# Six slots for weight pieces instead of four: the low part is written over the raw weights, and TensorE frees the slot

## The chip, the cores and the metric

The kernel runs on one core of a Trainium2 chip. The metric is the device time of one execution in microseconds (us). Five engines run their own instruction streams beside each other and meet only at semaphores: TensorE (PE, with its weight load PEld), VectorE (DVE), ScalarE (ACT), GpSimd (POOL) and SyncE (SP), which here issues nearly all DMA transfers. On-chip memory (SBUF) has 128 partitions.

## The reference

Two decoder layers on 256 tokens of width 2048, all in float32. Cut to what matters, one layer is:

```
h = rms_norm(x, norm_mix) * (1 + sc_a) + sh_a        # sc, sh, gates: c_act @ ada_w + ada_b
cq, ckv, ... = split(h @ w_in)                       # one wide projection
o_mla, o_fox, o_nsa = three attention mixers         # nsa also compresses k and v:
                                                     #   gelu(blocks @ cmp_w1) @ cmp_w2
x = x + gt_a * (concat(rms_norm(o_...)) @ w_out)
h = rms_norm(x, norm_mlp) * (1 + sc_m) + sh_m
x = x + gt_m * (square(relu(h @ mlp_w1)) @ mlp_w2)   # d_ff = 8192
```

Every weight is read once, so the kernel streams some 630 MB from HBM past a small activation (256 tokens).

## The kernel before, in words

**Pieces.** All large weights are cut into 828 pieces of 256 rows by up to 512 columns (512 KB), 414 for each layer: 158 for the attention part (`ORDER`, line 38 on) and 256 for the MLP. `PIECES` lists them in the order in which TensorE uses them. A float32 product is made of three products in the fp32r format: each weight piece is split into a high part `w_hi` (a rounding copy) and a low part `w_lo` (raw minus high), and the activations are split in the same way.

**The life of piece Q.** SP loads it into `w_raw[Q % RING]` (`load_piece`, lines 591 to 610). ACT makes `w_hi` (`hi`, line 713) once the load has landed and TensorE has used piece Q - RING (`piece_used`). DVE makes `w_lo` (`lo`, line 1150) once `hi_done` says so. TensorE multiplies (`product`, line 1600: 12 matmuls in most pieces; `compress`, line 1642: 4 matmuls for the pieces called `cw1`), then raises `piece_used`. RING is 4, and each of `w_raw`, `w_hi` and `w_lo` has four slots of its own. The raw slot is free again when `lo` of piece Q - 4 is done (`lo_done`, line 608).

**Side work in a written order.** ACT runs `hi(Q)` and then the side steps listed for Q, DVE runs `lo(Q)` and then its side steps for Q: turning transposed blocks out of PSUM, softmax units (`slot`), evacuations, residuals, and the adaLN modulation. A transpose that TensorE does behind piece Q is taken out at Q + 3 (`t_step` calls with `F + q + 3`), so at such places ACT and DVE cannot be more than some three pieces ahead of TensorE. Within the side steps of one Q the adaLN tile comes last (priority 5 in `ada_block`).

**The adaLN tiles.** `c_act @ ada_w` has one row, and DVE does it: 384 tiles of 128 x 1024 raw values (512 KB each) are loaded by SP and added into `ada_acc` (line 1092). The first 64 use eight slots in `arena`, the rest two slots `ada_raw`; a tile's load waits until DVE has used the tile two before it (`ada_used`). In the attention part of layer 0 and in its MLP the tiles are dense, later they are few, and in the attention part none stands behind a `cw1` piece.

**SP's queue.** SP issues weight and tile loads from one list, `LOADS` (lines 361 to 372), in order and blocking: a load that waits holds back all behind it. The list is sorted by the place in DVE's order at which the load's buffer comes free: for piece Q that is `lo` of Q - 4, for a tile the tile two before it.

**Stages.** Start (norm of layer 0 and its first chunks, with 64 tiles): up to about 182 us. The stretch with the `cw1` pieces, which alternate with others: 182 to 346 us in layer 0 and 1430 to 1582 us in layer 1. The rest of the attention part follows each. MLP of layer 0: some 579 to 1330 us. MLP of layer 1: from some 1810 us to the end.

Of the kernel before, what the change touches and what calls it, by code (L numbers as in the profile page):

```python
# [6 lines left out]
F32 = mybir.dt.float32  # L7
F32R = mybir.dt.float32r
# [5 lines left out]
P = 128  # L14
# [42 lines left out]
SUPERS = 4  # L57
MLP_LEN = SUPERS * 64
LAYER = FRONT + MLP_LEN
RING = 4  # L60
ALL = LAYERS * LAYER


# [294 lines left out]
assert len(ADA_LAST) == len(ADA_BLOCKS)  # L358


DVE_AT = {e: i for i, e in enumerate(DVE_ORDER)}
LOADS = []
for Q in range(ALL):
    free = DVE_AT["lo", Q - RING] if Q >= RING else DVE_AT["ada", 8 + Q]
    LOADS.append((free, DVE_AT["lo", Q], "w", Q))
for n in range(TILES):
    if n < FIRST_TILES:
        free = DVE_AT["ada", n - FIRST_RING] if n >= FIRST_RING else -1
    else:
        free = DVE_AT["ada", n - 2] if n >= FIRST_TILES + 2 else DVE_AT["ada", n - FIRST_RING]  # L370
    LOADS.append((free, DVE_AT["ada", n], "ada", n))
LOADS.sort()
# [34 lines left out]
def trunk(nc, x, c, positions, inv_freq, ada_w, ada_b, norm_mix, norm_mlp, w_in, fox_b_f, mla_q_norm, mla_w_uq,  # L407
          mla_kv_norm, mla_w_ukv, nsa_pos_k, nsa_pos_v, cmp_k_w1, cmp_k_w2, cmp_v_w1, cmp_v_w2,
          out_norm, w_out, mlp_w1, mlp_w2, final_norm, out):
    with ExitStack() as ctx:  # L410
        def sb(name, shape, dt=F32):
            return ctx.enter_context(nc.sbuf_tensor(name, shape, dt))

        def sem(name):
            return ctx.enter_context(nc.semaphore(name))
# [2 lines left out]
        X = sb("X", [P, 2, D])  # L418
        hT_hi, hT_lo = sb("hT_hi", [P, KT, SEQ], F32R), sb("hT_lo", [P, KT, SEQ], F32R)
        uT_hi, uT_lo = sb("uT_hi", [P, KT, SEQ], F32R), sb("uT_lo", [P, KT, SEQ], F32R)  # L420
        w_raw = sb("w_raw", [P, RING, 2, 512])
        w_hi, w_lo = sb("w_hi", [P, RING, 2, 512], F32R), sb("w_lo", [P, RING, 2, 512], F32R)
        ada_raw = sb("ada_raw", [P, 2, 1024])
        ada_acc = sb("ada_acc", [P, 1024])
        ybuf = sb("ybuf", [P, 2, 2, 512])
# [77 lines left out]
        packed, c_landed, loaded, consts, x_landed = sem("packed"), sem("c_landed"), sem("loaded"), sem("consts"), sem("x_landed")  # L503
        raw_landed = [sem(f"raw_landed{i}") for i in range(RING)]
        hi_done, lo_done, piece_used = sem("hi_done"), sem("lo_done"), sem("piece_used")
# [83 lines left out]
        @block.sync  # L589
        def _(sp):  # L590
            def load_piece(Q):
                l, chunk, p = PIECES[Q]
                if type(chunk) is not str:
                    s, ch = chunk
                    if ch < 4:
                        src = mlp_w1[l, 256 * p:256 * p + 256, s * D + 512 * ch:s * D + 512 * ch + 512]
                    else:
                        src = mlp_w2[l, s * D + 256 * p:s * D + 256 * p + 256, 512 * (ch - 4):512 * (ch - 4) + 512]
                    n = 512
                elif chunk == "cw1":  # L600
                    w1, n = (cmp_k_w1, cmp_v_w1)[p // 16], 512
                    src = w1[l, 256 * (p % 16):256 * (p % 16) + 256, :]
                else:
                    w, c0, n, a_ = CHUNKS[chunk]
                    row = P * OUT_KT[p] if w == "w_out" else 256 * p
                    src = w_rows[w][l, row:row + 256, c0:c0 + n]
                if Q >= RING:
                    sp.wait_ge(lo_done, Q - RING + 1)
                sp.dma_start(w_raw[:, Q % RING, :, 0:n], src.rearrange("(k p) n -> p k n", p=P)
                             ).then_inc(raw_landed[Q % RING], 16)  # L610

            def load_ada(n):
                l, kind, b = ADA_BLOCKS[n // KT]
                w = ada_w[l, P * (n % KT):P * (n % KT) + P, :]
                if kind in "AM":
                    part = 0 if kind == "A" else 3
                    src = w.rearrange("r (s d) -> r s d", s=6)[:, part:part + 2, 512 * b:512 * b + 512]
                else:
                    part = 2 if kind == "G" else 5
                    src = w[:, part * D + 1024 * b:part * D + 1024 * b + 1024].rearrange("r (s d) -> r s d", s=2)  # L620
                if n < FIRST_TILES:
                    if n >= FIRST_RING:
                        sp.wait_ge(ada_used, n - FIRST_RING + 1)
                    sp.dma_start(first_raw[:, n % FIRST_RING, :].rearrange("p (s d) -> p s d", s=2), src
                                 ).then_inc(first_landed[n % FIRST_RING], 16)
                else:
                    if n >= FIRST_TILES + 2:
                        sp.wait_ge(ada_used, n - 1)
                    sp.dma_start(ada_raw[:, n % 2, :].rearrange("p (s d) -> p s d", s=2), src
                                 ).then_inc(ada_landed[n % 2], 16)  # L630

            for free, needed, what, n in LOADS:
                if what == "w":
                    load_piece(n)
                else:
                    load_ada(n)
            for m in range(2):
                for j in (2, 0, 1, 3):
                    sp.wait_ge(out_act if j < 2 else out_dve, 2 * m + j % 2 + 1)
                    sp.dma_start(out_dram[:, m, 512 * j:512 * j + 512], X[:, m, 512 * j:512 * j + 512]).then_inc(stored, 16)  # L640
            sp.wait_ge(stored, 128)
# [1127 lines left out]
```

## Time and profile before

| | us |
|---|---|
| three runs | 2528.32, 2533.32, 2536.24 |
| median | 2533.32 |
| the profiled execution, its own time | 2532.85 |
| its span, first to last instruction | 2530.7 |

| engine | busy us | share of the span |
|---|---|---|
| PE | 2396.0 | 95% |
| PEld | 1972.4 | 78% |
| DVE | 1786.5 | 71% |
| ACT | 1193.7 | 47% |
| 16 DMA engines, SP's queue | | 74.9% |

The span is the stretch between the first and the last instruction of one profiled execution. Matmuls are pipelined and their ends are modelled, so the busy share of PE overstates how hard it works; its idle time is nevertheless idle. A row of waits names the waiting instruction, what released it, the total in us, how often and the longest one. A row of a stage gives the busy time of PE, PEld, DVE, ACT and POOL in this order, each with its count of instructions in brackets; where one line alone is asked for, only its engine stands there.

### The profile page before, as it was taken

Reading aid. Unit: us, or ns where it says so; the run is one execution under the profiler, and the core shown is the slowest. Engines: PE = TensorE matmul, PEld = TensorE weight load, DVE = VectorE, ACT = ScalarE, POOL = GpSimd, SP = SyncE. Lnnn points to the kernel's source line nnn. Section 1 sums busy time; section 2 is a strip of 40 time slices with the busy share of each in tenths; the row PEclk is TensorE's granted clock in tenths of the full one; section 3 lists DMA queues with packets and bytes.
Section 4 is the critical chain, followed back from the end, with each engine's and each line's share of the span. In section 5 each row is a group of like instructions: output and inputs, shape, how many; then the busy total and the mean of one; then the engine's idle time right before and its main releaser. Section 6 shows DMA issues by size and latency. Waiting matters only on the chain.

```text
span 2530.7 us, 29682 instructions
## 1 busy us (share of the span) xinstructions
PE 2396.0 (95%) x11277; PEld 1972.4 (78%) x11277; DVE 1786.5 (71%) x2152; ACT 1193.7 (47%) x1626; POOL 23.1 (1%) x48
## 2 busy tenths in 40 slices
PE   3799899989999999999999998999999999999998
PEld 3677678767778888888888877877788888888887
DVE  7888888777777777777777777676566545545555
ACT  3355544545534534434445555454554454453443
POOL 1000000000000000000000000000000000000000
PEclk9799999999999999999999999999999999999999
DMA  9979787688889889989877777466577666666664
GB/s 368 369 245 306 260 282 220 216 288 274 286 302 320 307 287 319 303 291 320 296 250 259 252 258 247 142 207 218 161 254 255 186 183 191 192 186 195 185 189 152
DMA packets 318612, 633.91 MB, mean 250 GB/s; under 512 B 20428, under 2 KB 41352, under 8 KB 317832
## 3 DMA queue, kind: packets, MB, share of 16 engines
q1 hardware_dynamic: 314432, 625.49, 74.9%
q10 hardware_dynamic: 4040, 6.54, 0.8%
q8 instruction: 90, 1.47, 0.2%
q14 instruction: 50, 0.41, 0.1%
HBM read 629.85 MB, written 2.10 MB: 250 GB/s over the span
## 4 chain that ended last, share of the span: by engine, by line
PE 61%; DVE 17%; DMA 11%; issue 5%; ACT 4%; SPq 0%; POOL 0%; ACTq 0%; DVEq 0%; POOLq 0%
PE acc L1634 14%; PE acc L1636 14%; PE acc L1635 14%; DMA ada_raw<-in_ada_w 7%; DVE w_lo L1152 6%; DVE ada_acc L1092 6%; PE pair L1634 5%; PE pair L1636 5%; PE pair L1635 5%; ACT w_hi L717 2%; DMA arena<-in_ada_w 1%; PE bank_T L1545 1%; PE bank_T L1500 1%; DMA w_raw<-in_nsa_cmp_k_w 1%; DMA w_raw<-in_nsa_cmp_v_w 1%
## 5 line engine op out<-in xcount | busy, mean ns | idle before, releaser
L1152 DVE TENSOR_TENSOR w_lo<-w_raw,w_hi 128x1024 fp32r<-128x1024 f32 (+3 forms) x828 | 979.5, 1192 | 378.3 <-ACT w_hi L717 376.8
L717 ACT ACTIVATE w_hi<-w_raw 128x1024 fp32r<-128x1024 f32 (+3 forms) x828 | 847.8, 1033 | 794.9 <-PE acc L1636 326.4
L1634 PE MATMUL acc<-w_hi,hT_hi 128*128 128x512 f32 (+3 forms) x1536 | 611.8, 398 | 39.2 <-DVE hT_lo L1286 16.4
L1636 PE MATMUL acc<-w_lo,hT_hi 128*128 128x512 f32 (+3 forms) x1536 | 590.5, 384 | 0.0
L1635 PE MATMUL acc<-w_hi,hT_lo 128*128 128x512 f32 (+3 forms) x1536 | 590.0, 384 | 0.0
L1092 DVE SCALAR_TENSOR_TENSOR ada_acc<-ada_raw,silu_c,ada_acc 128x1024 f32<-128x1024 f32 x300 | 384.2, 1281 | 108.6 <-DMA ada_raw<-in_ada_w 106.9
L1634 PEld LDWEIGHTS acc<-w_hi,hT_hi 128*128 128x128 f32 x1536 | 292.3, 190 | 108.2 <-DVE w_lo L1152 22.6
L1636 PEld LDWEIGHTS acc<-w_lo,hT_hi 128*128 128x128 f32 x1536 | 291.9, 190 | 56.6
L1635 PEld LDWEIGHTS acc<-w_hi,hT_lo 128*128 128x128 f32 x1536 | 292.8, 191 | 51.3 <-issue 1.7
L1634 PE MATMUL acc<-w_hi,uT_hi 128*128 128x512 f32 (+1 forms) x720 | 283.3, 394 | 0.8 <-DVE w_lo L1152 0.7
L1636 PE MATMUL acc<-w_lo,uT_hi 128*128 128x512 f32 (+1 forms) x720 | 279.6, 388 | 0.0
L1635 PE MATMUL acc<-w_hi,uT_lo 128*128 128x512 f32 (+1 forms) x720 | 279.4, 388 | 0.0
L1634 PE MATMUL pair<-w_hi,hT_hi 128*128 128x512 f32 (+1 forms) x448 | 178.5, 399 | 16.0 <-DVE w_lo L1152 16.0
L1636 PE MATMUL pair<-w_lo,hT_hi 128*128 128x512 f32 (+1 forms) x448 | 173.9, 388 | 0.0
L1635 PE MATMUL pair<-w_hi,hT_lo 128*128 128x512 f32 (+1 forms) x448 | 173.6, 387 | 0.0
L1634 PEld LDWEIGHTS acc<-w_hi,uT_hi 128*128 128x128 f32 x720 | 135.2, 188 | 29.8 <-DVE w_lo L1152 2.3
L1635 PEld LDWEIGHTS acc<-w_hi,uT_lo 128*128 128x128 f32 x720 | 135.3, 188 | 27.7 <-issue 1.0
L1636 PEld LDWEIGHTS acc<-w_lo,uT_hi 128*128 128x128 f32 x720 | 135.1, 188 | 27.8
L1634 PE MATMUL pair<-w_hi,uT_hi 128*128 128x512 f32 (+1 forms) x352 | 137.0, 389 | 2.2 <-DVE w_lo L1152 2.2
L1636 PE MATMUL pair<-w_lo,uT_hi 128*128 128x512 f32 (+1 forms) x352 | 136.2, 387 | 0.0
L1635 PE MATMUL pair<-w_hi,uT_lo 128*128 128x512 f32 (+1 forms) x352 | 136.2, 387 | 0.0
L1634 PEld LDWEIGHTS pair<-w_hi,hT_hi 128*128 128x128 f32 x448 | 85.6, 191 | 35.9 <-DVE w_lo L1152 20.3
(259 smaller groups left out, 2039.4 us busy)
## 6 DMA issues: line engine op xcount, KB each, us to landing
w_raw<-in_mlp_w SPq DMA_DIRECT2D x512, 512.0 KB, 4.8
ada_raw<-in_ada_w SPq DMA_DIRECT2D x320, 512.0 KB, 5.0
w_raw<-in_w_in SPq DMA_DIRECT2D x112, 512.0 KB, 4.9
arena<-in_ada_w SPq DMA_DIRECT2D x64, 512.0 KB, 11.0
w_raw<-in_w_out SPq DMA_DIRECT2D x64, 512.0 KB, 5.0
w_raw<-in_nsa_cmp_k_w SPq DMA_DIRECT2D x32, 512.0 KB, 5.0
w_raw<-in_nsa_cmp_v_w SPq DMA_DIRECT2D x32, 512.0 KB, 4.9
w_raw<-in_w_in SPq DMA_DIRECT2D x16, 388.0 KB, 4.0
```

The costliest lines, as they stand in the source:

```text
L717: a.activation(w_hi[:, Q % RING, :, 0:n], w_raw[:, Q % RING, :, 0:n], ACT.Copy).then_inc(hi_done, 1)
L1092: ins = v.scalar_tensor_tensor(ada_acc[:], raw, silu_c[:, kt:kt + 1], ada_acc[:], ALU.mult, ALU.add)
L1152: v.tensor_tensor(w_lo[:, Q % RING, :, 0:n], w_raw[:, Q % RING, :, 0:n], w_hi[:, Q % RING, :, 0:n].bitcast(F32), ALU.subtract).then_inc(lo ...
L1500: mm = pe.transpose(bank[:, k, P * m:P * m + P], halves[m], ident[:])
L1545: mm = pe.matmul(flat_[:, k:k + 1], ada_acc[:, P * k:P * k + P], ones[:, 0:1], start=True, stop=True)
L1634: pe.matmul(o, st_hi[:, kt + k, tok], wh, start=first and k == 0, stop=False)
L1635: pe.matmul(o, st_lo[:, kt + k, tok], wh, start=False, stop=False)
L1636: mm = pe.matmul(o, st_hi[:, kt + k, tok], wl, start=False, stop=last and k == 1)
```

## The change

`RING` goes from 4 to 6. `w_lo` and `w_raw` become one tensor: `w_raw` is allocated and released again at once, so that `w_lo` of the same size takes its place (12 slots of 4 KB a partition before, 4 for each of the three, and 12 after, 6 for each of two). `lo(Q)` now reads the raw values and writes the low part over them. SP therefore may load piece Q only when TensorE has used piece Q - 6 (`piece_used`), and ACT's wait for `piece_used` is also six pieces back. In the sorted list of loads, piece Q now stands where DVE does `lo` of Q - 3, one place later than before; the first six pieces stand at the tiles 8 to 13.

```
-RING = 4
+RING = 6
...
 for Q in range(ALL):
-    free = DVE_AT["lo", Q - RING] if Q >= RING else DVE_AT["ada", 8 + Q]
+    free = DVE_AT["lo", Q - RING + 3] if Q >= RING else DVE_AT["ada", 8 + Q]
...
-        w_raw = sb("w_raw", [P, RING, 2, 512])
-        w_hi, w_lo = sb("w_hi", [P, RING, 2, 512], F32R), sb("w_lo", [P, RING, 2, 512], F32R)
+        with nc.sbuf_tensor("w_raw", [P, RING, 2, 512], F32) as w_raw:
+            pass
+        w_lo = sb("w_lo", [P, RING, 2, 512], F32R)
+        w_hi = sb("w_hi", [P, RING, 2, 512], F32R)
...
                 if Q >= RING:
-                    sp.wait_ge(lo_done, Q - RING + 1)
+                    sp.wait_ge(piece_used, Q - RING + 1)
                 sp.dma_start(w_raw[:, Q % RING, :, 0:n], ...).then_inc(raw_landed[Q % RING], 16)
```

No instruction is added or removed on ACT, DVE or TensorE.

## Rows read from the trace of the kernel before

**Rows 1.** The page's first line.

```profile
span 2530.7 us, 29682 instructions
```

**Rows 2.** Busy time by stage: stretch, length, busy us (instructions), PEclk, DMA share, GB/s.

```profile
34.00:182.00 148.00, 122.67 (x556) 105.93 (x557) 127.41 (x175) 62.23 (x94) 1.39 (x2) 0.86 0.92 325
182.00:346.00 164.00, 143.86 (x736) 115.87 (x735) 135.90 (x208) 83.39 (x133) 0.69 (x1) 0.99 0.86 288
...
579.00:760.00 181.00, 174.03 (x782) 139.62 (x783) 140.34 (x139) 87.91 (x106) 0.56 (x1) 1.00 0.85 288
760.00:1330.00 570.00, 567.11 (x2604) 469.06 (x2602) 429.46 (x395) 254.90 (x277) 0.54 (x1) 1.00 0.88 299
...
1430.00:1582.00 152.00, 139.31 (x725) 114.48 (x724) 119.10 (x192) 84.76 (x135) 0.69 (x1) 1.00 0.78 258
...
1810.00:2525.00 715.00, 711.34 (x3204) 587.77 (x3204) 399.73 (x358) 334.81 (x368) 0.90 (x2) 1.00 0.63 196
```

**Rows 3.** Waits of PE, 182 to 346 us: total us, times, longest.

```profile
PE acc L1654 <- DVE w_lo L1152: 8.6, 7, 1.8
PE acc L1634 <- DVE w_lo L1152: 4.4, 5, 2.0
```

**Rows 4.** Waits of PE, 1430 to 1582 us.

```profile
PE acc L1654 <- DVE w_lo L1152: 8.4, 8, 2.4
PE acc L1634 <- DVE w_lo L1152: 2.2, 3, 1.1
```

**Rows 5.** Waits of DVE, 182 to 346 us.

```profile
DVE w_lo L1152 <- ACT w_hi L717: 20.9, 22, 2.5
```

**Rows 6.** Waits of DVE, 1430 to 1582 us.

```profile
DVE w_lo L1152 <- ACT w_hi L717: 26.6, 23, 3.0
```

**Rows 7.** Waits of ACT, 760 to 1330 us.

```profile
ACT w_hi L717 <- DMA w_raw<-in_mlp_w: 125.6, 67, 4.0
ACT w_hi L717 <- PE acc L1636: 90.9, 65, 3.5
```

**Rows 8.** SP in order of time, 204 to 219 us: start, us, instruction.

```profile
205.62 0.37 SPq L609 DMA_DIRECT2D w_raw<-in_nsa_cmp_k_w  x1
206.96 0.37 SPq L609 DMA_DIRECT2D w_raw<-in_w_in  x1
208.16 0.37 SPq L629 DMA_DIRECT2D ada_raw<-in_ada_w  x1
209.61 0.37 SPq L609 DMA_DIRECT2D w_raw<-in_nsa_cmp_k_w  x1
```

**Rows 9.** DVE in order of time, the same stretch.

```profile
204.36 2.57 DVE L1152 TENSOR_TENSOR w_lo<-w_raw,w_hi 128x1024 fp32r<-128x1024 f32 x2 [2.51 <-ACT w_hi L717]
206.85 1.28 DVE L1092 SCALAR_TENSOR_TENSOR ada_acc<-ada_raw,silu_c,ada_acc 128x1024 f32<-128x1024 f32 x1
```

**Rows 10.** PE in order of time, 200 to 204.5 us.

```profile
202.88 0.40 PE L1655 MATMUL acc<-w_lo,uT_hi 128*128 128x512 f32 x1
```

**Rows 11.** Weight loads of 182 to 346 us, issue to landing.

```profile
DMA to landing us min/median/max: 3.1/5.3/8.0
```

**Rows 12.** Line 1152 by stage: stretch, length, DVE busy (instructions), PEclk, DMA share, GB/s.

```profile
182.00:346.00 164.00, 73.11 (x66) 0.99 0.86 288
```

**Rows 13.** Line 1092 (the tiles) by stage, same columns.

```profile
182.00:346.00 164.00, 34.37 (x27) 0.99 0.86 288
...
1430.00:1582.00 152.00, 16.62 (x13) 1.00 0.78 258
```

**Rows 14.** DVE groups by form: count, busy us, mean ns, idle before.

```profile
L1152 DVE TENSOR_TENSOR w_lo<-w_raw,w_hi 128x1024 fp32r<-128x1024 f32 x756 | 918.6, 1222 | 362.7 <-ACT w_hi L717 361.3
...
L1281 DVE TENSOR_TENSOR X<-X,ybuf 128x1024 f32<-128x1024 f32 x36 | 44.1, 1225 | 1.2
```

**Rows 15.** ACT groups by form.

```profile
L717 ACT ACTIVATE w_hi<-w_raw 128x1024 fp32r<-128x1024 f32 x756 | 794.9, 1057 | 753.9 <-PE acc L1636 314.8 <-DMA w_raw<-in_mlp_w 179.3 <-PE pair L1636 136.3
```

**Rows 16.** Weight loads of 760 to 1330 us, issue to landing.

```profile
DMA to landing us min/median/max: 2.9/5.6/9.8
```

## The prediction

> **What bounds the kernel now.** I read the busy time by stage first. The two MLPs are closed: PE is busy 567.11 of 570 us in layer 0 and 711.34 of 715 us in layer 1 [rows 2]. Together they are half of the span [rows 1], and nothing that feeds TensorE better can gain there; a change can only lose. The idle time is elsewhere: 148 - 122.67 = 25.3 us at the start, 164 - 143.86 = 20.1 us and 152 - 139.31 = 12.7 us in the two stretches with `cw1` pieces, 181 - 174.03 = 7.0 us in the first part of layer 0's MLP [rows 2]. So the `cw1` stretches hold 32.8 us that could go.
>
> Then I asked who ends PE's waits there. It is the low part: 8.6 + 4.4 = 13.0 us in layer 0 [rows 3], 8.4 + 2.2 = 10.6 us in layer 1 [rows 4]. DVE in its turn waited for the high part for 20.9 us [rows 5] and 26.6 us [rows 6], and was busy 135.90 of 164 and 119.10 of 152 us [rows 2]: it is nearly the bound itself, and each time it sits waiting for a late load it loses time that it can't win back before TensorE needs the piece.
>
> In the MLP of layer 0 the same question has another answer: ACT waits half for landings (125.6 us) and half for TensorE to free `w_hi` (90.9 us for one accumulator alone) [rows 7], and PE sees neither.
>
> **The change part by part.** Work on the engines stays as it is; what moves are the times of loads and how far conversions may run ahead.
>
> *In place subtraction.* DVE already has a subtraction-like form with the output over an input: `X<-X,ybuf`, 128 x 1024, 1225 ns, against 1222 ns for the low part into its own tensor [rows 14]. I take 0. Ends: -3 to +3 ns on each of 756, ±2 us, and only where DVE is late.
>
> *The gate of a load.* Before, a raw slot cycles in landing 5.3 [rows 11] + high part 1.06 [rows 15] + low part 1.22 [rows 14] = 7.6 us for four pieces, 1.9 us a piece. The layer 0 stretch runs at 164 / 66 = 2.48 us a piece [rows 12]; the loop alone isn't the bound, but one late landing (8.0 at most [rows 11]) closes the 2.3 us that four pieces have to spare. After, a slot also holds the piece until TensorE is through: 12 matmuls at 711.34 / 3204 = 0.222 us [rows 2] are 2.7 us, four are 0.9 us. That is 8.5 to 10.3 us for six pieces, at most 1.7 us a piece, and 4.6 us to spare in six. So the new gate by itself is looser.
>
> *The place in SP's queue.* SP blocks in order, and piece Q now stands behind `lo` of Q - 3. If DVE has a tile behind `lo` of Q - 4, the load of the next tile but one stands ahead of piece Q and waits for that tile. One case in full: SP issued a `cw1` piece at 205.62, the next piece at 206.96, a tile at 208.16 and the next `cw1` piece at 209.61 [rows 8]; DVE did two low parts from 204.36 on and a tile from 206.85 to 208.13 [rows 9]. The first of these loads needed the first low part (205.6). After, it needs the piece six before it, which TensorE left at 202.88 + 0.40 = 203.3 [rows 10]: 2.3 us earlier. The second now stands behind the tile's load: 208.2 or later in place of 206.96, 1.3 us later. So a tile makes one load 1.28 us later, and the others may come earlier by one turn of DVE, 1.22 us at the least.
>
> Counted: layer 0 has 27 tiles on 66 pieces [rows 12, 13], so 27 x 1.28 = 34.6 us later against 39 x 1.22 = 47.6 us earlier, in all -13.0 us or -0.2 us a load. Layer 1 has 13 tiles [rows 13] on as many pieces: 16.6 against 53 x 1.22 = 64.7 us, -48.1 us or -0.7 us a load. DVE's waits shrink by that where they were waits for a landing: 22 x 0.2 = 4.4 us and 23 x 0.7 = 16 us. PE gains what it was itself waiting: 13.0 / 20.9 = 0.6 of the first and 10.6 / 26.6 = 0.4 of the second, 2.7 and 6.4 us. Since the earlier half is only allowed where TensorE isn't late itself, and loads issued together land later, I take about half: -1.5 us (ends -13.0 and +6, the latter if the pieces behind tiles set the pace: 7.6 + 1.28 = 8.9 us for four, 2.2 us a piece, which leaves 0.26 us a piece against 2.48) and -4 us (ends -10.6 and +2).
>
> *What waits behind a load that now waits for TensorE.* Behind it in SP's queue stand tile loads, and behind those DVE, in order. A tile's load needs a tile that DVE does two tiles later in its order, and I assume that DVE is less than six pieces ahead of TensorE, so that the tile's own wait is the later one. I take 0; the end is in the slow rival.
>
> *MLP of layer 0.* A load now waits for Q - 6 to be used, in place of the low part of Q - 4. Seen from TensorE at 2.7 us a piece, a slot's six pieces last 16.3 us; the landing takes 5.6 [rows 16], a tile ahead of it 1.3, the conversions 2.3, the product 2.7: 11.9 us, 4.4 us to spare. Before, the high part could start 4 x 2.7 = 10.9 us before the end of its product, and 10.9 - 2.3 - 2.7 = 5.9 us were to spare. DVE's bursts are a residual of two operations of 1.22 us, a split and a tile, about 4.4 us. It just fits. I take +1.5 us (ends 0 and +12). What hides this is the lead that DVE has at 429.46 of 570 us busy [rows 2]; if it were gone, each late landing (67 waits [rows 7]) would show.
>
> The Trainium skill (DMA: Bandwidth & Descriptors, Rules for kernel authors) says to issue a DMA early, compute, and wait for it late. That rule speaks against this edit in the MLPs, where loads move later; the rows of this stage show 4.4 us of cover left, and by them the rule costs 0 to 12 us.
>
> *Start.* DMA engines are at 0.92 of the time there [rows 2], with 64 tiles and some 36 pieces to bring. Pieces now stand one turn later behind three or four tiles, so tiles, which DVE is waiting for, come a transfer or so sooner: 0.5 MB at 325 GB/s [rows 2] is 1.6 us. I take -1 (ends -3 and +4).
>
> *MLP of layer 1 and everything else.* Conversions may run six ahead in place of four, but transposes are taken out three pieces behind their issue, so ACT and DVE are held to TensorE as before: 0 (ends -3 and +3).
>
> Sum: -1.5 - 4 + 1.5 - 1 = -5 us. The profiled execution's own time is 2532.85 us, its span 2530.7 [rows 1] and 2.2 around it, and it lies 0.5 us under the median of 2533.32. 2532.85 - 5 = 2527.9: **2528 us**.
>
> **The rivals.**
>
> *The `cw1` stretches open up.* For: 47.5 us of DVE's waiting for the high part [rows 5, 6], and a DVE that is near its bound, so that what it saves adds up from piece to piece. Against: 40 tiles in the two stretches still push loads back. If two thirds of the 32.8 us of idle time go, -22 us, with +1.5 elsewhere: 2512 us. The Trainium skill (Perfetto Trace Analysis, Optimization Strategy) says that the same gap repeating on the engine that should be full can mean too few buffers. That the gaps of rows 3 and 4 repeat agrees with it; the deeper ring would then give what this rival gives.
>
> *Nothing moves.* For: order lists hold ACT and DVE to three pieces of TensorE, and pieces in flight fall from eight (four raw, four converted) to six. Then 2533 us: the change doesn't do what it says.
>
> *Slower: the total depth of six is too little in layer 0's MLP.* Its place is 579 to 1330 us. After a burst DVE regains ground at the speed of its loads: behind a tile (5.6 + 1.06 + 1.22 + 1.28) / 4 = 2.29 us a piece against 2.7, before it was 1.97. Of 5.9 us of cover 4.4 are left; from the point where a burst is longer than that, each group of eight pieces leaves a gap. With 751 us / (8 x 2.9 us) = 32 groups and 0.4 us each that is +13 us: 2545 us. For it speaks that ACT waits 67 times for a landing already [rows 7]; against it, that PE stands only 2.9 us in 570 now.
>
> **How the numbers follow.** A measurement can tell about 0.3%, 7.6 us, from no change. The forecast has 0.28, the open stretches 0.26, nothing moves 0.18, the slow rival 0.20; 0.08 is for what I don't see, both ways. Of the forecast's own range, 2518 to 2535, a quarter lies below 2525.7. Faster: 0.26 + 0.07 + 0.03 = 0.36. Slower: 0.20 + 0.03 = 0.23. Same: 0.41. The range goes from 2510, short of the fast rival's far end, to 2546, the slow one's value.
>
> **What would show it.** Waits of PE on `w_lo` in the `cw1` stretches fall from 13.0 to about 11 and from 10.6 to about 6 us; DVE's waits for `w_hi` fall more in layer 1 than in layer 0. ACT's waits on PE before `w_hi` nearly vanish in both MLPs, and its waits for landings take their place. PE stays within 3 us of full in layer 1's MLP and loses 1 to 2 us in layer 0's. The low part keeps 1.22 us. I am wrong if the layer 0 stretch gains as much as layer 1's (then SP's order doesn't matter), if PE gets gaps of microseconds in the MLP of layer 0, or if DVE's waits for tiles grow, which would mean that SP stands blocked on TensorE.

## The result: half a per cent slower

| | median us | runs | lowest to highest |
|---|---|---|---|
| before | 2535.45 | 15 | 2528.32 to 2539.72 |
| after | 2547.18 | 15 | 2537.11 to 2551.89 |

The ratio is 1.005, with a 95% interval of 1.0039 to 1.006: 11.7 us slower, 19 us off the forecast of 2528 and just above the end of its range, 2546. The spans of the two profiled executions stand 19.2 us apart, and a part of that is TensorE's clock in just these two. The mean granted clock is 0.987 in before's trace and 0.981 in after's, while the means over all runs are 0.983 for both (15 runs of after; 23 of before beside the first experiments). After's own runs go from 2537.11 us at 0.985 to 2551.89 at 0.981, and that last one is the profiled one. So a stage is compared below by TensorE's idle time first, and by its length second.

Of after, the page's first line and its line for all low parts, and then the line for the high parts of full size:

```profile
span 2549.9 us, 29680 instructions
...
L1156 DVE TENSOR_TENSOR w_lo<-w_raw,w_hi 128x1024 fp32r<-128x1024 f32 (+3 forms) x828 | 975.8, 1192 | 400.0 <-ACT w_hi L721 397.4
```

```profile
L721 ACT ACTIVATE w_hi<-w_raw 128x1024 fp32r<-128x1024 f32 x756 | 787.9, 1056 | 689.2 <-DMA w_raw<-in_mlp_w 531.7 <-DMA w_raw<-in_w_in 74.2 <-DMA w_raw<-in_w_out 39.0
```

ACT's waits for TensorE [rows 15] are all but gone (5.6 us over the whole execution) and landings have taken their place, for the MLP's weights 179.3 us before and 531.7 now. That is what was meant. Next the same work by stage, with bounds moved to after's own stages: three lines of after to set beside [rows 2] (stretch, length, busy us of PE, PEld, DVE, ACT, POOL with counts, PEclk, DMA share, GB/s):

```profile
184.70:355.80 171.10, 147.75 (x738) 119.27 (x737) 136.09 (x208) 84.53 (x134) 0.69 (x1) 0.97 0.81 278
...
1441.00:1598.00 157.00, 143.00 (x722) 117.40 (x721) 119.10 (x198) 82.24 (x132) 0.69 (x1) 0.98 0.74 250
1830.00:2544.00 714.00, 711.06 (x3204) 587.40 (x3203) 392.40 (x357) 328.70 (x367) 0.71 (x2) 1.00 0.65 198
```

The `cw1` stretches are 7.1 and 5 us longer. DVE is as busy as before in them (136.09 and 119.10 us), so it stands idle longer. The MLP of layer 1 is as it was.

A cleaner cut goes by pieces. The bounds here are the times at which TensorE was through with piece 17, 101, 157, 413 and 515: layer 0 from piece 18 on with all its `cw1` pieces, the rest of its attention part, its MLP, and layer 1 down to its last `cw1` piece. Before:

```profile
122.61:346.19 223.58, 198.81 (x1008) 162.71 (x1007) 183.92 (x303) 116.83 (x185) 2.08 (x3) 0.98 0.82 275
346.19:578.84 232.65, 219.07 (x1090) 175.77 (x1089) 182.88 (x287) 107.90 (x200) 1.93 (x3) 0.99 0.74 243
578.84:1328.81 749.97, 741.14 (x3384) 608.67 (x3384) 569.51 (x533) 341.81 (x381) 1.09 (x2) 1.00 0.87 297
1328.81:1579.06 250.25, 230.94 (x1212) 195.59 (x1213) 192.03 (x305) 139.21 (x220) 2.62 (x4) 1.00 0.78 256
```

After:

```profile
120.60:355.84 235.24, 203.98 (x1008) 166.68 (x1007) 185.91 (x305) 117.85 (x186) 2.08 (x3) 0.96 0.77 263
355.84:594.98 239.14, 224.16 (x1090) 179.53 (x1089) 182.70 (x287) 107.18 (x200) 1.93 (x3) 0.96 0.71 237
594.98:1339.83 744.85, 739.49 (x3384) 610.56 (x3384) 573.96 (x533) 340.73 (x381) 1.09 (x2) 1.00 0.88 299
1339.83:1598.01 258.18, 236.25 (x1212) 199.49 (x1213) 191.92 (x305) 139.12 (x220) 2.63 (x4) 0.98 0.74 247
```

The counts of PE are the same line by line. Lengths grow by 11.7, 6.5, -5.1 and 7.9 us. TensorE's idle time (length less busy) goes from 24.8 to 31.3, 13.6 to 15.0, 8.8 to 5.4 and 19.3 to 21.9 us, in all from 66.5 to 73.5. The other 13.9 us are the same matmuls taking longer at a lower granted clock (0.96, 0.96 and 0.98 against 0.98, 0.99 and 1.00 in the three stages that lose), and 7.5 us of this belong to the two executions, which stand 19.2 us apart where the medians stand 11.7. In the second stage the slower matmuls are 5.1 of the 6.5 us. So the change added idle time where the `cw1` pieces are and took some away in layer 0's MLP.

**What is late.** SP in order of time in the `cw1` stretch of after (start, us, instruction):

```profile
192.22 0.37 SPq L613 DMA_DIRECT2D w_raw<-in_nsa_cmp_k_w  x1
198.92 0.37 SPq L633 DMA_DIRECT2D ada_raw<-in_ada_w  x1
199.33 0.47 SPq L613 DMA_DIRECT2D w_raw<-in_mla_w_ukv  x1
199.84 0.47 SPq L613 DMA_DIRECT2D w_raw<-in_nsa_cmp_k_w  x1
202.38 0.37 SPq L633 DMA_DIRECT2D ada_raw<-in_ada_w  x1
202.80 0.47 SPq L613 DMA_DIRECT2D w_raw<-in_w_in  x1
203.31 0.49 SPq L613 DMA_DIRECT2D w_raw<-in_nsa_cmp_k_w  x1
```

The same place before:

```profile
194.95 0.37 SPq L609 DMA_DIRECT2D w_raw<-in_mla_w_ukv  x1
196.14 0.37 SPq L629 DMA_DIRECT2D ada_raw<-in_ada_w  x1
197.28 0.37 SPq L609 DMA_DIRECT2D w_raw<-in_nsa_cmp_k_w  x1
```

Before, the `ukv` piece went out ahead of the tile. After, it stands behind the tile's load, and SP stands for 6.7 us, from 192.22 to 198.92, until DVE has done the tile two before. DVE in order of time shows what lies in those 6.7 us: a low part, ten side steps, another low part, and only then the tile (from 197.61):

```profile
192.82 1.22 DVE L1156 TENSOR_TENSOR w_lo<-w_raw,w_hi 128x1024 fp32r<-128x1024 f32 x1
193.96 0.42 DVE L1226 COPY ybuf<-pair 128x256 f32<-128x256 f32 x1
...
196.48 1.22 DVE L1156 TENSOR_TENSOR w_lo<-w_raw,w_hi 128x1024 fp32r<-128x1024 f32 x1
197.61 1.28 DVE L1096 SCALAR_TENSOR_TENSOR ada_acc<-ada_raw,silu_c,ada_acc 128x1024 f32<-128x1024 f32 x1
...
205.75 1.23 DVE L1156 TENSOR_TENSOR w_lo<-w_raw,w_hi 128x1024 fp32r<-128x1024 f32 x1 [2.25 <-ACT w_hi L721]
```

TensorE had left the slot in question (line 1640, the last matmul of the piece six before) at 196.16 + 0.39 = 196.55. The load was free to go and went 2.8 us later, at 199.33. So for the first 4.3 of SP's 6.7 us this slot wasn't free either, and 2.8 us is what the place in the list cost this load. What came of it, first on ACT, then on PE:

```profile
204.66 1.06 ACT L721 ACTIVATE w_hi<-w_raw 128x1024 fp32r<-128x1024 f32 x1 [4.19 <-DMA w_raw<-in_mla_w_ukv]
205.62 0.58 ACT L768 ACTIVATE arena<-bank_T 128x512 f32<-128x512 f32 x1
```

```profile
196.16 0.39 PE L1640 MATMUL acc<-w_lo,hT_hi 128*128 128x512 f32 x1
...
206.25 0.44 PE L1504 MATMUL bank_T<-ident,ybuf 128*128 128x128 f32 x2 [1.37 <-ACT arena L768]
```

ACT sat 4.19 us for the landing. Its copy out of `bank_T` is queued behind the high part, so it was late too, and for that copy PE stood 1.37 us. This is one late load, end to end. The bracket on PE's row names line 768 as the releaser, and only ACT's row above it shows that a DMA was behind it.

### The profile page after: what moved, and what is told of

Its sections match the earlier page's. It is cut to its first block, busy times and chain, and to the rows that moved or that the text cites. A ratio compares the mean times of both kernels' runs of the same rounds, so it can differ in the third digit from the quotient of the medians.

```text
span 2549.9 us, 29680 instructions
## 1 busy us (share of the span) xinstructions
PE 2406.3 (94%) x11277; PEld 1982.6 (78%) x11277; DVE 1785.2 (70%) x2152; ACT 1185.4 (46%) x1626; POOL 23.0 (1%) x48
## 4 chain that ended last, share of the span: by engine, by line
PE 67%; DVE 14%; DMA 10%; ACT 4%; issue 4%; SPq 1%; POOL 0%; ACTq 0%; DVEq 0%; POOLq 0%
PE acc L1638 15%; PE acc L1640 15%; PE acc L1639 15%; PE pair L1638 5%; PE pair L1640 5%; PE pair L1639 5%; DVE ada_acc L1096 5%; DVE w_lo L1156 4%; DMA w_raw<-in_w_in 4%; DMA ada_raw<-in_ada_w 3%; ACT w_hi L721 2%; PE bank_T L1549 1%; DMA arena<-in_ada_w 1%; PE bank_T L1504 1%; PE bank_O L1504 1%
## 5 line engine op out<-in xcount | busy, mean ns | idle before, releaser
L1156 DVE TENSOR_TENSOR w_lo<-w_raw,w_hi 128x1024 fp32r<-128x1024 f32 (+3 forms) x828 | 975.8, 1192 | 400.0 <-ACT w_hi L721 397.4
L721 ACT ACTIVATE w_hi<-w_raw 128x1024 fp32r<-128x1024 f32 (+3 forms) x828 | 841.3, 1032 | 762.5 <-DMA w_raw<-in_mlp_w 531.7
L1096 DVE SCALAR_TENSOR_TENSOR ada_acc<-ada_raw,silu_c,ada_acc 128x1024 f32<-128x1024 f32 x300 | 383.9, 1280 | 60.2 <-DMA ada_raw<-in_ada_w 59.2
```

The lines of the kernel that those rows point to most:

```text
L721: a.activation(w_hi[:, Q % RING, :, 0:n], w_raw[:, Q % RING, :, 0:n], ACT.Copy).then_inc(hi_done, 1)
L1096: ins = v.scalar_tensor_tensor(ada_acc[:], raw, silu_c[:, kt:kt + 1], ada_acc[:], ALU.mult, ALU.add)
L1156: v.tensor_tensor(w_lo[:, Q % RING, :, 0:n], w_raw[:, Q % RING, :, 0:n], w_hi[:, Q % RING, :, 0:n].bitcast(F32), ALU.subtract).then_inc(lo ...
```

## The experiments

Each ratio is against the kernel before on the same chip, with its 95% interval. Diffs are against after, or against before where it says so.

**1 to 4: the two halves of the change apart.** The change does two things to a load: it may go only when TensorE has used Q - 6, and it stands one place later in SP's list. First the changed kernel with the old place:

```
-    free = DVE_AT["lo", Q - RING + 3] ...
+    free = DVE_AT["lo", Q - RING + 2] ...
```

> The changed kernel with the load of piece Q sorted at the low part of Q - 4 (as before the change) in place of Q - 3; in-place ring of six and TensorE's gate stay. Theory A (the loss comes from the place in SP's queue: a load stands behind a tile's load and waits for that tile): the 19 us lost before layer 0's MLP and in layer 1's attention part go, 2530 to 2536 us in all. Theory B (the loss comes from the new gate, six pieces until TensorE is through in place of four raw and four converted): stays at 2545 us or more. Theory C (order lets TensorE's gate hold back tile loads): DVE's waits for tiles grow beyond the 59 us of the changed kernel, time between the two.

Measured: 2528.38 us (12 runs, 2521.03 to 2537.01) against 2536.75, ratio 0.9969 (0.9956 to 0.9981). The loss is gone, and a small gain is left. SP in the same stretch of this kernel:

```profile
188.48 0.37 SPq L613 DMA_DIRECT2D w_raw<-in_nsa_cmp_k_w  x1
192.83 0.37 SPq L613 DMA_DIRECT2D w_raw<-in_mla_w_ukv  x1
195.19 0.37 SPq L633 DMA_DIRECT2D ada_raw<-in_ada_w  x1
195.60 0.47 SPq L613 DMA_DIRECT2D w_raw<-in_nsa_cmp_k_w  x1
```

The `ukv` piece leaves at 192.83, ahead of the tile again, and 4.3 us after the load ahead of it; in after that gap was 7.1 us (192.22 to 199.33). The time lies a little below the 2530 us at which theory A's range begins, and theory B is out.

One place earlier still (`Q - RING + 1`):

> The same with the load of piece Q sorted at the low part of Q - 5, one place earlier still. Theory A: no tile stands ahead of a load that could go, 2525 to 2535 us. Theory B: 2545 us or more. Theory C: SP now often stands blocked on TensorE with tile loads behind it, DVE waits for tiles over 120 us in all, and the time is above that of the run with Q - 4, 2535 to 2545 us.

Measured: 2595.05 us (5 runs, 2593.39 to 2600.24), ratio 1.0236 (1.0218 to 1.0254). This is the opposite fault: loads now stand ahead of their time and SP waits for TensorE, with the tiles behind it. The waits for tiles grew as theory C said (212.0 us), but the time lies 50 us above its range, so what this costs was far underrated. Theory B names the same times for another reason, and the old place had already ruled it out. SP in this kernel, in layer 0's MLP:

```profile
1000.11 8.53 SPq L613 DMA_DIRECT2D w_raw<-in_mlp_w  x4
1008.68 0.47 SPq L633 DMA_DIRECT2D ada_raw<-in_ada_w  x1
```

and DVE, which needed that tile:

```profile
1007.14 1.28 DVE L1096 SCALAR_TENSOR_TENSOR ada_acc<-ada_raw,silu_c,ada_acc 128x1024 f32<-128x1024 f32 x1
1008.33 1.22 DVE L1156 TENSOR_TENSOR w_lo<-w_raw,w_hi 128x1024 fp32r<-128x1024 f32 x1
1013.89 1.28 DVE L1096 SCALAR_TENSOR_TENSOR ada_acc<-ada_raw,silu_c,ada_acc 128x1024 f32<-128x1024 f32 x1 [4.34 <-DMA ada_raw<-in_ada_w]
```

Four weight loads go out in 8.53 us, (8.53 - 0.37) / 3 = 2.72 us apart, which is TensorE's own pace for a piece, and the tile's load comes only after them. DVE had done the tile two before it at 1006.09, so SP held this load back for 2.6 us. DVE stood 4.34 us.

The order alone, with the four slots of the kernel before (diff against before):

```
-    free = DVE_AT["lo", Q - RING] ...
+    free = DVE_AT["lo", Q - RING + 1] ...
```

> The kernel before (four slots each, gate on the low part of Q - 4) with its loads sorted one place later, at the low part of Q - 3: the change's order alone. Theory A: it takes most of the loss, 2543 to 2555 us. Theory B: 2534 to 2538 us.

Measured: 2553.17 us (5 runs, 2551.68 to 2558.99), ratio 1.0068 (1.0052 to 1.0084). That is theory A's range.

The gate alone, with old slots and old order (against before, ahead of each weight load):

```
+                if Q >= 6:
+                    sp.wait_ge(piece_used, Q - 6 + 1)
```

> The kernel before with one wait more on SP ahead of each weight load, for TensorE to have used piece Q - 6: the change's gate alone, order as before. Theory A: within 4 us of the kernel before, 2532 to 2540 us. Theory B: 2543 us or more. Theory C: waits of DVE for tiles grow from 107 us, since tile loads stand behind the gate, 2536 to 2542 us.

Measured: 2544.00 us (12 runs, 2538.45 to 2547.57), ratio 1.0031 (1.002 to 1.0043). By its time this is theory B's range: with four slots the gate alone does cost something. But the table of stages below puts that cost into layer 0's MLP (14.8 us of idle time against 8.8) and hardly into the stage where after loses most (25.8 against 24.8). So the gate isn't what made after slow.

DVE's waits over the whole execution separate these kernels (total us, times, longest). The order alone:

```profile
DVE w_lo L1152 <- ACT w_hi L717: 450.9, 408, 5.4
DVE ada_acc L1092 <- DMA ada_raw<-in_ada_w: 55.3, 66, 2.9
```

The gate alone:

```profile
DVE w_lo L1154 <- ACT w_hi L719: 373.6, 334, 3.6
DVE ada_acc L1094 <- DMA ada_raw<-in_ada_w: 131.6, 96, 4.4
```

| us DVE waits for | high part | tile |
|---|---|---|
| before | 376.8 | 106.9 |
| after | 397.4 | 59.2 |
| old place | 323.9 | 112.1 |
| one place earlier | 304.0 | 212.0 |
| order alone | 450.9 | 55.3 |
| gate alone | 373.6 | 131.6 |

The first column says how late weights come, the second how late tiles come. The later a weight load stands in the list, the better for tiles and the worse for weights. The gate adds to the waits for tiles.

**5: what the ring's gain is made of.** Old place, six slots, but ACT may make the high part only when TensorE has used Q - 4, as before:

```
-                if Q >= RING:
-                    act.wait_ge(piece_used, Q - RING + 1)
+                if Q >= 4:
+                    act.wait_ge(piece_used, Q - 4 + 1)
```

> The run sorted at Q - 4, but ACT makes the high part only when TensorE has used piece Q - 4 (as before the change) in place of Q - 6: raw weights still have six slots, the lead of the conversions is four again. Theory D (what the ring gives is the longer lead of ACT and DVE): the gain goes, 2540 to 2548 us, as in the kernel before with the gate alone. Theory E (it gives the earlier loads): 2526 to 2532 us.

Measured: 2531.13 us (12 runs, 2524.3 to 2534.24) against 2534.77, ratio 0.9984 (0.9974 to 0.9994). This is theory E's range, and the ratio stays far below that of the gate alone (1.0031). The two differ in that a load here needn't wait for `lo` of Q - 4, so most of what the six slots bring is the earlier load. The longer lead of the conversions is worth some 0.15%, by which this ratio and that of the old place differ; their intervals overlap, so it may be nothing.

**6 and 7: tiles in a queue of their own.** If SP's order is the trouble, a second issuing engine should end it. All tile loads from tile 64 on were moved to GpSimd's list, with the same waits, on the changed kernel and on the one before:

```
...
+            root(0)
+            for kind, n in POOL_ORDER:
+                if kind == "root":
+                    root(n)
+                else:
+                    load_ada(gp, n)
```

> The changed kernel with the tile loads from tile 64 on issued by GpSimd in a list of its own (its square roots stand between them in DVE's order), so that no weight load stands behind a tile and no tile behind TensorE's gate. Theory A with C (the shared blocking queue costs): 2515 to 2530 us, DVE's waits for tiles below 100 us. Theory B (the gate): 2545 us or more. If GpSimd's issue is slow, tiles land later and DVE's waits for them exceed 150 us.

> The kernel before with the same move of the tile loads to GpSimd: it shows what the queue alone is worth with four slots. Theory A: little, 2528 to 2538 us, since with the place at Q - 4 no load waits for a tile that stands behind it; the run with six slots is then 8 us or more faster than this one.

Measured: 2567.92 us (4 runs, 2565.74 to 2575.71), ratio 1.0139 (1.0121 to 1.0157), and 2566.80 (4 runs, 2564.18 to 2570.49), ratio 1.013 (1.0117 to 1.0143). Both times lie far above what theory A gave. The first is in the range that was named for the gate (2545 us or more), but the old place has the same gate and gains. GpSimd in order of time, changed kernel with the tiles moved:

```profile
901.39 0.72 POOL L620 DMA_DIRECT2D ada_raw<-in_ada_w  x1 [2.74 <-DVE ada_acc L1115]
906.09 0.72 POOL L620 DMA_DIRECT2D ada_raw<-in_ada_w  x1 [3.97 <-DVE ada_acc L1115]
```

and DVE's waits for tiles over the whole execution, just short of the 150 us named for a slow issue:

```profile
DVE ada_acc L1115 <- DMA ada_raw<-in_ada_w: 147.4, 105, 5.8
```

GpSimd takes 0.72 us where SP takes 0.37 to 0.47. From the records of each tile, a load goes 0.32 us (mean) after its slot is free, where SP's goes after 0.05 in after and 0.03 in before. It then lands in 5.5 us against 4.7 in after, and with four slots in 5.3 against 5.1 in before (medians 5.5 and 4.6, 5.0 and 5.0). With two slots for tiles that delay shows where tiles are dense. By stage the moved tiles still say something for the theory: in the pieces 18 to 101, where after has 31.3 us of idle time, the changed kernel with tiles moved has 21.3 (table below). It loses in the next two stages, and the kernel with four slots does too. Whether all of it comes from the later issue and landing, or some from the steps of `POOL_ORDER` that stand between tiles, was not taken apart. In total time the pair doesn't tell ring and queue apart.

**8 to 10: the place, chosen by stage.** If the order acts locally, places can be mixed. Late place only in layer 0's MLP, old place elsewhere:

```
+    free = DVE_AT["lo", Q - RING + (3 if FRONT <= Q < LAYER else 2)] ...
```

> The ring of six with the load of piece Q sorted at the low part of Q - 4, except in the MLP of layer 0 (pieces 158 to 413), where the change's place at Q - 3 stays. If the place in the queue costs where TensorE is starved and helps where SP would stand blocked on TensorE with tile loads behind it: layer 0's MLP takes about 5 us less than in the kernel before, the rest as in the run sorted at Q - 4, 2522 to 2528 us. If the stages are coupled through something else: 2528 us or more.

Measured: 2523.11 us (8 runs, 2520.23 to 2531.11) against 2534.77, ratio 0.9963 (0.995 to 0.9975): the best of all and as expected, though its interval overlaps that of the old place throughout. The waits of DVE for tiles are those of the late place:

```profile
DVE ada_acc L1096 <- DMA ada_raw<-in_ada_w: 56.3, 66, 5.7
```

Old place only for the pieces 18 to 101 of each layer, late place elsewhere, and then old place only for the pieces 102 to 157:

```
+    free = DVE_AT["lo", Q - RING + (2 if 18 <= Q % LAYER < 102 else 3)] ...
```

> The changed kernel with the place at Q - 4 only for the pieces 18 to 101 of each layer's attention part (the stretch with the cw1 pieces and the run-up to it), Q - 3 elsewhere. If the losses of the stages are due to the order in each stage itself and add up, this takes back what was lost there, about 11 us in layer 0 and 7 us in layer 1: 2528 to 2534 us. If the losses sit elsewhere: 2540 us or more.

```
+    free = DVE_AT["lo", Q - RING + (2 if 102 <= Q % LAYER < FRONT else 3)] ...
```

> The changed kernel with the place at Q - 4 only for the pieces 102 to 157 of each layer (the rest of the attention part, with a tile behind nearly every piece of layer 0), Q - 3 elsewhere. If the stages add up: about 4 us back in layer 0, nothing in layer 1, 2541 to 2546 us.

Measured: 2528.24 us (12 runs, 2522.91 to 2539.6) against 2536.3, ratio 0.9968 (0.9956 to 0.9981), and 2542.88 (11 runs, 2538.43 to 2545.35), ratio 1.0026 (1.0016 to 1.0035). Both came as expected. Against after's 1.005, undoing the place where the `cw1` pieces are takes away 0.82%, the whole loss and more; undoing it in the rest of the attention part takes away 0.24%. The sum is 1.06%; less the 2.3 us or 0.09% of idle time that the late place saves in layer 0's MLP against the old one (7.7 and 5.4 us) it is 0.97%, beside the 0.81% between after and the old place throughout, with intervals of about 0.12% a side. So within the noise the stages act by themselves.

TensorE's idle time by stage in us, the mean granted clock of the profiled execution, and what the medians differ by:

| kernel | 18-101 | 102-157 | 158-413 | 414-515 | sum | clock | median, against before |
|---|---|---|---|---|---|---|---|
| before | 24.8 | 13.6 | 8.8 | 19.3 | 66.5 | 0.987 | |
| after (late place) | 31.3 | 15.0 | 5.4 | 21.9 | 73.5 | 0.981 | +11.7 |
| old place | 20.9 | 11.3 | 7.7 | 17.7 | 57.7 | 0.982 | -8.4 |
| one place earlier | 21.7 | 22.0 | 37.1 | 15.7 | 96.5 | 0.977 | +58.3 |
| order alone, four slots | 29.8 | 14.5 | 5.4 | 24.7 | 74.3 | 0.984 | +16.4 |
| gate alone, four slots | 25.8 | 13.1 | 14.8 | 18.9 | 72.5 | 0.986 | +7.2 |
| lead of four | 23.4 | 12.5 | 9.0 | 18.6 | 63.5 | 0.985 | -3.6 |
| after, tiles on GpSimd | 21.3 | 18.7 | 24.3 | 17.6 | 81.8 | 0.980 | +33.2 |
| before, tiles on GpSimd | 22.8 | 17.1 | 25.0 | 18.0 | 83.0 | 0.981 | +32.0 |
| late in layer 0's MLP only | 22.3 | 13.8 | 5.1 | 19.4 | 60.7 | 0.983 | -11.7 |
| old in 18-101 only | 21.1 | 13.3 | 6.9 | 17.0 | 58.3 | 0.985 | -8.1 |
| old in 102-157 only | 28.0 | 11.8 | 5.2 | 21.5 | 66.6 | 0.981 | +6.6 |

Down the first column: 28.0 to 31.3 us wherever the late place holds in SP's queue, with four slots or six; 20.9 to 23.4 with six slots and the old place; 24.8 before. In the third, the late place has 5.1 to 6.9 us and the old one 7.7 to 9.0, but 14.8 with the gate alone. The fourth column goes as the first does. Each cell is one execution, and cells that should be alike differ by up to some 3 us (28.0 and 31.3). The sum of the idle time orders the kernels nearly as the medians do.

## Why the prediction was wrong

It said 2528, and that the time would fall by 5 us. It rose by 11.7. The sum holds the mechanism, SP's order, but with the wrong size and so with the wrong sign.

**The step that failed is "The place in SP's queue".** It said that a tile makes one load 1.28 us later and that the others come at least 1.22 us earlier, in all -0.2 us a load in layer 0 and -0.7 in layer 1. From the records of each piece, means in us over a stage:

| | pieces | issue after `lo` of Q - 4 | issue after use of Q - 6 | issue to landing | landing to `lo` |
|---|---|---|---|---|---|
| before | 18-101 | 0.02 | 2.05 | 5.35 | 4.21 |
| after | 18-101 | 0.68 | 2.79 | 6.14 | 3.24 |
| old place | 18-101 | -0.73 | 0.90 | 5.74 | 4.48 |
| before | 102-157 | 0.02 | -0.26 | 5.10 | 10.25 |
| after | 102-157 | 3.20 | 2.69 | 5.25 | 7.28 |
| before | 158-413 | 0.02 | -0.44 | 5.56 | 4.88 |
| after | 158-413 | 2.08 | 1.13 | 5.74 | 2.56 |

Where I had -0.2 us a load, loads of pieces 18 to 101 went 0.66 us later and took 0.79 us longer to land. In layer 1, pieces 432 to 515, where I had -0.7, they went 0.08 us later (0.11 after `lo` of Q - 4, 0.03 before) and took 0.51 us longer (5.27, 4.76).

Both terms of the step were mis-sized. The same records of after, split by whether a tile stands between the piece's two places (in before every load goes out as soon as `lo` of Q - 4 is done):

| pieces | a tile between | loads | issue after `lo` of Q - 4 |
|---|---|---|---|
| 18-101 | yes | 39 | 2.22 |
| 18-101 | no | 45 | -0.63 |
| 432-515 | yes | 22 | 2.25 |
| 432-515 | no | 62 | -0.65 |

So a tile makes a load 2.2 us later and not 1.28, and the others come 0.66 us earlier and not 1.22 or more. The late half is longer because side steps of DVE stand between `lo` of Q - 4 and the tile: in before the tile is done 2.17 us after that `lo` in the mean of these 39. I had picked a case [rows 8, 9] in which nothing lay between. SP's issue of the tile's own load comes on top, 198.92 to 199.33 in the case above. The early half is only half there, and after a tile's load two weight loads go out back to back (199.33 and 199.84; 202.80 and 203.31) whose slots had been free. The 2.05 us by which slots were free sooner, which the ring has to offer, help only in a list that lets the loads go: they grow to 2.79 with the late place and fall to 0.90 with the old one.

What hung on the step fell with it. DVE's waits for the high part were to shrink by 4.4 and 16 us in the two `cw1` stretches, from 20.9 and 26.6 us [rows 5, 6]. They grew. Of after, 184.7 to 355.8 us and then 1441 to 1598 us:

```profile
DVE w_lo L1156 <- ACT w_hi L721: 28.6, 22, 3.4
```

```profile
DVE w_lo L1156 <- ACT w_hi L721: 30.0, 22, 3.5
```

That it is the order is shown by the order alone (1.0068) and by the old place (0.9969), on either side of 1. In these stages the forecast had -1.5 and -4 us; idle time rose by 6.5 and 2.6.

**Layer 0's MLP** I took at +1.5 us, and it lost 3.5 us of idle time (8.83 to 5.36). Loads went 2.1 us later there, as the step said, and the cover held. What I missed is the other side of the exchange. Tiles now leave ahead of weights, and DVE's waits for them fell in this stage. Of before, 760 to 1330 us, and then of after, 776 to 1340 us:

```profile
DVE ada_acc L1092 <- DMA ada_raw<-in_ada_w: 70.7, 41, 4.4
```

```profile
DVE ada_acc L1096 <- DMA ada_raw<-in_ada_w: 35.1, 39, 3.1
```

The gain is the order's (5.4 us idle with the order alone too), and little of it the ring's (7.7 with the old place, against 8.8). The rule of the Trainium skill (DMA: Bandwidth & Descriptors, Rules for kernel authors) that a DMA be issued early was weighed for weights only, at 0 to 12 us; what the trace shows is that it counted for tiles.

**The rest of the attention part** I took at 0, within 3 us. By idle time that holds, +1.4. But it wasn't free: a tile stands between the two places for 50 of 56 pieces there (39 of 84 in 18-101), loads went 3.2 us later, and putting back the old place there alone takes the ratio from 1.005 to 1.0026. The idle time of this stage says less: 11.3 and 11.8 us in two kernels with the old place there and 15.0 in after, but 13.8 in another with the old place (late in layer 0's MLP only) and 13.3 in one with the late place (old in 18-101 only). I hadn't counted tiles there.

**The rival on the slower side** gave 2545 us, near the 2547.18 measured, but for a wrong reason. It put the loss between 579 and 1330 us, where time was gained. That it came so near is luck.

**"What waits behind a load that now waits for TensorE"** I took at 0, and in after that holds: waits for tiles fell over the whole execution, 106.9 to 59.2 us. But it holds because of the late place. With the gate alone something costs 0.31%, and one place earlier it is the 2.4% of that kernel. The late place guards the tiles against the new gate at a price in late weights, and the price is too high: with the old place the waits for tiles are 112.1 us, little more than before, and the kernel is faster.

**What was right.** The subtraction in place costs nothing: the 756 full low parts mean 1222 ns before [rows 14] and after:

```profile
L1156 DVE TENSOR_TENSOR w_lo<-w_raw,w_hi 128x1024 fp32r<-128x1024 f32 x756 | 914.1, 1222 | 373.1 <-ACT w_hi L721 370.7
```

ACT's waits on PE turned into waits for landings. The MLP of layer 1 didn't move. Through piece 17 the kernel was 2.0 us ahead of before, where -1 had been forecast for the start; the twelve traces scatter between 120.0 and 125.4 us there, so this shows no more than that the start didn't lose. The waits of PE on `w_lo` in the two stretches, forecast to fall from 13.0 and 10.6 us, did not fall, but they don't hold the loss either. Of after, 184.7 to 355.8 us and then 1441 to 1598 us:

```profile
PE acc L1658 <- DVE w_lo L1156: 7.0, 6, 1.7
PE acc L1638 <- DVE w_lo L1156: 6.2, 6, 2.0
```

```profile
PE acc L1658 <- DVE w_lo L1156: 7.9, 7, 2.3
PE acc L1638 <- DVE w_lo L1156: 2.7, 4, 1.1
```

13.2 and 10.6 us beside 13.0 and 10.6 [rows 3, 4]. Some of the new idle time goes by other names, as PE's 1.37 us for line 768 above. A sum over one releaser was the wrong gauge for these stretches; the length less the busy time shows it.

**What stays open.** That the gate alone costs 6 us of idle time in layer 0's MLP because tile loads wait behind it is argued from DVE's waits for tiles (131.6 beside 106.9 us) and from the kernel one place earlier, not isolated. Something speaks against it: a tile's load goes 0.25 us (mean) after its slot is free with the gate alone and 0.32 us with the old place and six slots, which has no such loss (7.7 us of idle time). In the profiled pair idle time grew by 7.0 us, while the medians stand 11.7 us apart; what makes up the rest isn't shown. Whether idle time itself lowers the clock is open too: the three kernels with the late place throughout or in both `cw1` stretches have mean clocks over their runs of 0.982 to 0.983 and the old place 0.984, a difference too small for these runs.

## What to carry to other kernels

When two rings of buffers are loaded from one in-order queue that blocks, the position of a load in that queue is a tuning parameter as strong as the depth of the ring: here six slots in place of four gave -0.3% with the old order, +0.5% with an order one place later and +2.4% with one a place earlier. Price a move in such a queue by what stands between the two places on the engine that releases the neighbour, with all its side steps and waits, and count the neighbours in every stage. Where the stages differ, each can have its own place: weights first where the consumer of weights is tight, tiles first where it has cover. The kernel with late places in layer 0's MLP alone was the fastest here (0.9963), but the old place throughout (0.9969) lies within its interval.

## What the runs showed of the hardware

A queue's wait stands on the engine that issues, and all behind it stands too: SP was silent from 192.22 to 198.92 us, and the slot of its next weight load had been free since 196.55. The Trainium skill (DMA: Bandwidth & Descriptors, Anatomy of one DMA) says that DMA engines don't wait on semaphores and that the wait is made by the issuing sequencer before dispatch. The trace agrees.

Loads of pieces 18 to 101 landed later in after, 6.14 us against 5.35 in the mean of 84, while the stage as a whole moved fewer bytes a second (263 against 275 GB/s). In after 63 of them have a neighbour in SP's queue within 0.7 us, in before 12. But those 63 land no later than the other 21 (6.00 and 6.55 us), so that it is the issuing in pairs isn't shown. The prediction said without a number that loads issued together land later.

A second issuing engine was no remedy: GpSimd's issue takes 0.72 us in the rows above, the tiles land 0.9 us later (median 5.5 against 4.6) with six slots and no later (5.0 both) with four, and the kernels are 1.4% and 1.3% slower than before. The same page of the Trainium skill (Rules for kernel authors) says that spreading DMAs over issuing engines doesn't bring bandwidth and only saves issue time. Bandwidth didn't rise here (in layer 0's MLP 288 GB/s with the tiles on GpSimd, 299 in after), and GpSimd spent more time on each issue than SP had.
